# Decay factors of an mLSTM one step ahead, and an output projection that begins inside the last attention heads

## The reference, cut to what matters

```
# first block, mLSTM: 4 heads of 128 features, two directions (one direction shown)
qk  = einsum('bhcjd,bhcsd->bhcjs', q, k)
P   = exp(D - m_j[..., None]) * qk
num = einsum('bhcjs,bhcsd->bhcjd', P, v) + inter_w * einsum(C_prev, q)
h   = num / maximum(abs(den), exp(-m_j))
h   = h * rsqrt(mean(h * h) + EPS) * norm_g            # per head
# second block, forgetting attention: 16 heads of 64 features, causal
s = einsum('bhqd,bhkd->bhqk', q_i, k) * scale + c_i[..., None] - c
o = einsum('bhqk,bhkd->bhqd', softmax(where(kpos <= qpos, s, -inf)), v)
o = o * sigmoid(gate)
x = x + o @ b_w_out                                    # "bout" below
```

## Time and profile before

| | us |
|---|---|
| median of 3 runs (2162.28 to 2163.73) | 2163.47 |
| the profiled execution's own time | 2162.06 |
| its span, first to last instruction | 2160.3 |
| PE busy in the span | 2115.6 (98%) |
| POOL, DVE, ACT busy | 1208.9, 962.1, 881.5 |

### The profile page before, as it was taken

One profiled execution on the slowest core, in us unless ns is written; L12 is line 12 of the kernel. 1 busy time (PEld: TensorE's weight loads), 2 busy tenths in 40 slices (PEclk: granted clock), 3 DMA queues, 4 the chain that ended last, 5 costly groups with the idle time before them and its releaser, 6 DMA issues.

```text
span 2160.3 us, 29709 instructions
## 1 busy us (share of the span) xinstructions
PE 2115.6 (98%) x9884; PEld 1716.2 (79%) x9884; DVE 962.1 (45%) x1675; ACT 881.5 (41%) x1325; POOL 1208.9 (56%) x1601
## 2 busy tenths in 40 slices
PE   8999998999999999999999999999999989999999
PEld 6787877887888888888788888887777768888887
DVE  5557455335444442224445555115556554555400
ACT  5444456333443433332244343225545544444321
POOL 7454335778566565654556556566444436565653
PEclk9999999999999999999999999999999999999999
DMA  6233211333333323332333333333222213333332
GB/s 218 94 93 112 67 59 54 88 93 99 97 106 91 102 88 107 96 101 88 94 91 97 97 97 93 99 100 118 69 89 88 69 40 98 101 93 97 99 99 74
DMA packets 60827, 202.88 MB, mean 94 GB/s; under 512 B 6768, under 2 KB 6896, under 8 KB 60736
## 3 DMA queue, kind: packets, MB, share of 16 engines
q1 hardware_dynamic: 60624, 201.55, 30.8%
q10 hardware_dynamic: 112, 0.16, 0.0%
HBM read 199.42 MB, written 2.26 MB: 93 GB/s over the span
## 4 chain that ended last, share of the span: by engine, by line
PE 89%; DVE 4%; ACT 3%; DVEq 1%; issue 1%; ACTq 1%; POOL 1%; DMA 0%; SPq 0%; POOLq 0%
PE bank L1483 27%; PE bank L1485 27%; PE bank L1484 27%; PE bank L1734 1%; PE bank L1708 1%; PE bank L1720 1%; PE bank L1771 1%; ACTq L665 1%; PE bank L1772 1%; PE bank L1773 1%; PE bank L1527 1%; POOL WL L472 1%; PE bank L1752 1%; DMA X<-in_x 0%; ACT SX L664 0%
## 5 line engine op out<-in xcount | busy, mean ns | idle before, releaser
L472 POOL TENSOR_TENSOR WL<-RAW,WH 128x256 fp32r<-128x256 f32 x1496 | 1160.6, 809 | 893.9 <-ACT WH L579 893.3
L1483 PE MATMUL bank<-XH,WH 128*128 128x512 f32 x1816 | 715.5, 394 | 2.8 <-DVE VN L1196 2.5
L1485 PE MATMUL bank<-XH,WL 128*128 128x512 f32 x1816 | 707.9, 390 | 0.0
L1484 PE MATMUL bank<-XL,WH 128*128 128x512 f32 x1816 | 707.6, 390 | 0.0
L579 ACT ACTIVATE WH<-RAW 128x1024 fp32r<-128x1024 f32 x374 | 392.0, 1051 | 240.1 <-PE bank L1485 237.6
L1483 PEld LDWEIGHTS bank<-XH,WH 128*128 128x128 f32 x1816 | 341.3, 188 | 82.9 <-DVE FG L1402 4.5
L1485 PEld LDWEIGHTS bank<-XH,WL 128*128 128x128 f32 x1816 | 341.3, 188 | 71.6
L1484 PEld LDWEIGHTS bank<-XL,WH 128*128 128x128 f32 x1816 | 341.5, 188 | 71.1 <-issue 1.4
L1483 PE MATMUL bank<-FH,WH 128*128 128x512 f32 x528 | 205.4, 389 | 0.0
L1485 PE MATMUL bank<-FH,WL 128*128 128x512 f32 x528 | 205.4, 389 | 0.0
L1484 PE MATMUL bank<-FL,WH 128*128 128x512 f32 x528 | 205.4, 389 | 0.0
(11 more groups left out here) (274 smaller groups left out, 2373.6 us busy)
## 6 DMA issues: line engine op xcount, KB each, us to landing
RAW<-in_w_up SPq DMA_DIRECT2D x132, 512.0 KB, 3.6
RAW<-in_w_att SPq DMA_DIRECT2D x50, 512.0 KB, 3.6
RAW<-in_w_down SPq DMA_DIRECT2D x48, 448.0 KB, 3.3
RAW<-in_w_fa SPq DMA_DIRECT2D x32, 512.0 KB, 3.6
RAW<-in_w_down SPq DMA_DIRECT2D x24, 512.0 KB, 3.5
RAW<-in_w_ain SPq DMA_DIRECT2D x24, 512.0 KB, 3.6
RAW<-in_w_mrg SPq DMA_DIRECT2D x15, 512.0 KB, 3.6
RAW<-in_w_mrg SPq DMA_DIRECT2D x24, 256.0 KB, 2.6
```

Of the source, the lines that this page charges most:

```text
L472: last = nc.gpsimd.tensor_tensor(WL[:, s, w], RAW[:, s, w], WH[:, s, w].bitcast(F32), ALU.subtract)
L1483: mm(dst[:, 0:width], WH[:, s, w], a, start=start and k == 0, stop=False)
L1484: mm(dst[:, 0:width], WH[:, s, w], b, start=False, stop=False)
L1485: last = mm(dst[:, 0:width], WL[:, s, w], a, start=False, stop=stop and k == kc - 1)
```

## The change

1. `SXM` has its two tiles the other way round, and ACT makes the decay factors of step m+1 where it made those of step m. Those of step 0 are made in the slot of the last cross-attention step.
2. The last 128 columns of `bout` units 0 to 3 (their last part) go to tiles of their own, `WEH` (ACT) and `WEL` (POOL). ACT's `hi` for these units is two instructions, POOL's `lo` five. `bout_ends` reads the new tiles.
3. A new semaphore `bout_read` counts when part 6 of unit n has been read; ACT then copies units 4 to 7 (`hi_behind`) while the last pair is still in work. The residual no longer does it (`have = 5`).
4. PE's fillers are cut: unit 1 in parts 0-1 and 2-5, unit 2 in 0-2 and 3-6, unit 3 in 0-3 and 4-6, part 6 of units 0 and 1 earlier; the transposes of the last group stand ahead of unit 3, no longer behind it. Units 1 and 2 exchange their banks.
5. DVE: `o_gate` and `o_split` of pair 6 move behind the work of groups 0 and 1 of pair 7; ACT follows (`o_split`, and `out_gate` of pair 7 one group later). The first six `o_split` are dealt 4 and 2, no longer 3 and 3.

```
@@ -245,3 +245,3 @@
     EG = [at(f"EG{n}", k, [P, S]) for n, k in enumerate((74, 76, 78, 80, 82, 84, 54, 56, 58))]
-    SXM = [SX, at("SX1", 86, [P, 2, S])]
+    SXM = [at("SX1", 86, [P, 2, S]), SX]
@@ -267,2 +267,5 @@
     CD = at("CD", 86, [P, 2, 2, P])
+    WEH = at("WEH", 80, [P, 4, P], F32R)
+    WEL = at("WEL", 82, [P, 4, P], F32R)
+    KEND = (KB - 1) * P
@@ -312,3 +315,3 @@
     f_mask = sem("f_mask")
-    oh_ready, ol_ready = sem("oh_ready"), sem("ol_ready")
+    oh_ready, ol_ready, bout_read = sem("oh_ready"), sem("ol_ready"), sem("bout_read")
     out_done = sem("out_done")
@@ -359,3 +362,3 @@
-    BOUT = [bank[7], LB[(O["bout"] + 1) % 2], LB[O["bout"] % 2], bank[2], bank[3], bank[4], bank[5], bank[6]]
+    BOUT = [bank[7], LB[O["bout"] % 2], LB[(O["bout"] + 1) % 2], bank[2], bank[3], bank[4], bank[5], bank[6]]
@@ -553,8 +556,17 @@
                     f_masks((n - 6 - g) // 4, g)
-        lo(U["bout"], 0, 0, 0)
+        def lo_parted(n):
+
+            s = (U["bout"] + n) % NSLOT
+            pool.wait_ge(hi_ready, U["bout"] + n + 1)
+            for w in [slice(c * 2 * P, min((c + 1) * 2 * P, KEND)) for c in range(LO_PARTS)]:
+                nc.gpsimd.tensor_tensor(WL[:, s, w], RAW[:, s, w], WH[:, s, w].bitcast(F32), ALU.subtract)
+            nc.gpsimd.tensor_tensor(WEL[:, n, :], RAW[:, s, KEND:UW], WEH[:, n, :].bitcast(F32), ALU.subtract)\
+                .then_inc(lo_ready, 1)
+
+        lo_parted(0)
         f_masks(FA_LAST - 1, 2)
-        lo(U["bout"], 1, 0, 0)
-        lo(U["bout"], 2, 0, 0)
+        lo_parted(1)
+        lo_parted(2)
         f_masks(FA_LAST, 0)
-        lo(U["bout"], 3, 0, 0)
+        lo_parted(3)
         f_masks(FA_LAST, 1)
@@ -650,5 +662,6 @@
                        accum_out=RS[:, turn_of(g, j)]).then_inc(p_exp, 1)
-            if st and st[0] == "ml":
-                h, s = st[1], st[2]
-                m = 4 * h + s
+            m = 0 if st == LAST_STEP else 4 * st[1] + st[2] + 1 if st and st[0] == "ml" else 4 * ML_H
+            if m < 4 * ML_H:
+
+                h, s = m // 4, m % 4
                 if s == 0:
@@ -657,5 +670,5 @@
                     act.wait_ge(v_ready, VEV[("gate", 0)] + 1)
-                if m < 2:
+                if m == 1:
                     act.wait_ge(t_full, 2 * len(STEPS))
-                else:
+                elif m >= 2:
                     act.wait_ge(ms_read, m - 1)
@@ -750,3 +763,3 @@
                 for j in range(per):
-                    if not (at_end and j + AHEAD >= per) and not (have and i == 0 and j < have):
+                    if not (at_end and j + AHEAD >= per) and not (have and i * per + j < have):
                         hi(U[name], j + AHEAD, i, per)
@@ -834,2 +847,19 @@
+        def hi_parted(n):
+
+            s = (U["bout"] + n) % NSLOT
+            act.wait_ge(raw_full[s], 16 * ((U["bout"] + n) // NSLOT + 1))
+            act.wait_ge(unit_done, U["bout"] + n - NSLOT + 1)
+            if n == 0:
+                act.wait_ge(fc_out, 16)
+            A_(WH[:, s, 0:KEND], RAW[:, s, 0:KEND], ACT.Copy)
+            A_(WEH[:, n, :], RAW[:, s, KEND:UW], ACT.Copy).then_inc(hi_ready, 1)
+
+        def hi_behind(n):
+
+            s = (U["bout"] + n) % NSLOT
+            act.wait_ge(raw_full[s], 16 * ((U["bout"] + n) // NSLOT + 1))
+            act.wait_ge(bout_read, n - NSLOT + 1)
+            A_(WH[:, s, :], RAW[:, s, :], ACT.Copy).then_inc(hi_ready, 1)
+
         def squared(p, s):
@@ -881,6 +911,8 @@
             for s in range(4):
-                if p < FA_PAIRS:
+                if p < FA_PAIRS and 4 * p + s + AHEAD < 4 * FA_PAIRS:
                     hi(U["fa"], 4 * p + s + AHEAD, 0, 0)
+                elif p < FA_PAIRS:
+                    hi_parted(4 * p + s + AHEAD - 4 * FA_PAIRS)
                 elif s == 0:
-                    hi(U["bout"], AHEAD, 0, 0)
+                    hi_parted(AHEAD)
                 if p < FA_LAST and s >= 2:
@@ -891,7 +923,11 @@
                     head_rstd(FA_LAST, 1)
-                    o_split(FA_LAST - 1)
                 if p >= 1 and s < FA_G:
                     exps(p - 1, s)
-                if p >= 1 and s == 0:
+                if 1 <= p < FA_PAIRS and s == 0:
                     out_gate(p - 1)
+                if p == FA_PAIRS:
+                    if s == 0:
+                        o_split(FA_LAST - 1)
+                    for n in ((), (4, 5), (6,), (7,))[s]:
+                        hi_behind(n)
                 if p < FA_PAIRS and (s == 0 or s == (2 if p == FA_LAST else 1)):
@@ -903,4 +939,6 @@
                     turned(p - 1, s)
+                if p == FA_PAIRS and s == 1:
+                    out_gate(FA_LAST)
                 if p == FA_LAST and s >= 2:
-                    for n in range(3 * s - 6, 3 * s - 3):
+                    for n in range(4) if s == 2 else range(4, FA_LAST - 1):
                         o_split(n)
@@ -908,3 +946,3 @@
         fa_rounds(round_)
-        residual("bout", 2, 4, 4, "fg2", unrolled=lambda j: None, have=1)
+        residual("bout", 2, 4, 4, "fg2", unrolled=lambda j: None, have=KB - AHEAD)
         up("up2", 2, 11, ACT.Silu)
@@ -1417,4 +1455,2 @@
                 head_done(FA_LAST, 1)
-                o_gate(FA_LAST - 1)
-                o_split(FA_LAST - 1)
                 values_out(FA_LAST)
@@ -1422,3 +1458,7 @@
                     mins(FA_LAST, g)
+                    if g == 1:
+                        o_split(FA_LAST - 1)
                     shares(FA_LAST, g)
+                    if g == 0:
+                        o_gate(FA_LAST - 1)
                 o_gate(FA_LAST)
@@ -1767,3 +1807,3 @@
             for k in range(k0, k1):
-                if n == 0:
+                if n == 0 or k == FA_LAST - 1:
                     pe.wait_ge(ol_ready, k + 1)
@@ -1775,16 +1815,15 @@
                 last.then_inc(unit_done, 1)
+            elif k1 == KB - 1 and n < NSLOT:
+                last.then_inc(bout_read, 1)
-        def bout_ends(count):
+        def bout_ends():
             k = KB - 1
-            w = slice(k * P, (k + 1) * P)
             pe.wait_ge(oh_ready, KB)
-            for n in range(count):
-                slot = (U["bout"] + n) % NSLOT
-                mm(BOUT[n][:], WH[:, slot, w], AH[:, k, :], start=False, stop=False)
-                mm(BOUT[n][:], WL[:, slot, w], AH[:, k, :], start=False, stop=False)
+            for n in range(NSLOT):
+                mm(BOUT[n][:], WEH[:, n, :], AH[:, k, :], start=False, stop=False)
+                mm(BOUT[n][:], WEL[:, n, :], AH[:, k, :], start=False, stop=False)
             pe.wait_ge(ol_ready, KB)
-            for n in range(count):
-                slot = (U["bout"] + n) % NSLOT
-                mm(BOUT[n][:], WH[:, slot, w], AL[:, k, :], start=False, stop=True).then_inc(unit_done, 1)
+            for n in range(NSLOT):
+                mm(BOUT[n][:], WEH[:, n, :], AL[:, k, :], start=False, stop=True).then_inc(unit_done, 1)
@@ -1796,8 +1835,12 @@
                 f_turn(pp)
+                pe.wait_ge(lin_free, O["bout"] + 1)
+                bout(1, 0, 2)
                 f_scores(pp, 0)
-                pe.wait_ge(lin_free, O["bout"] + 2)
-                bout(1, 0, pp)
+                bout(1, 2, pp - 1)
                 f_transposes(pp, 0)
                 f_scores(pp, 1)
-                bout(2, 0, pp)
+                pe.wait_ge(lin_free, O["bout"] + 2)
+                bout(2, 0, 3)
+                bout(0, pp - 1, pp)
+                bout(1, pp - 1, pp)
                 f_products(pp, 0)
@@ -1805,9 +1848,10 @@
                 f_scores(pp, 2)
+                bout(2, 3, pp)
                 f_products(pp, 1)
-                pe.wait_ge(fs_read, 2 * FA_G * FA_PAIRS - 1)
-                bout(3, 0, pp)
                 f_transposes(pp, 2)
-                bout(0, pp - 1, pp)
+                pe.wait_ge(fs_read, 2 * FA_G * FA_PAIRS)
+                bout(3, 0, 4)
                 f_products(pp, 2)
-                bout_ends(4)
+                bout(3, 4, pp)
+                bout_ends()
                 pe.wait_ge(fo_free, FA_PAIRS)
```

## The result

| | before | after |
|---|---|---|
| median of 4 runs each, us | 2162.88 (2161.14 to 2163.73) | 2143.08 (2141.58 to 2143.14) |
| profiled execution, its span | 2162.06, 2160.3 | 2143.13, 2141.4 |

The ratio is 0.9906 (95% interval 0.9894 to 0.9918): 19.8 us or 0.94% faster. Predicted were 2143.9 us and a span of 2140.7.

The account below looks back on a forecast made before the run. PE bounds the kernel, busy 2115.6 of 2160.3 us, so only idle time can be won. 10.5 (mLSTM) and 9.1 (last pair) sum to 19.6 us: span 2140.7, median 2143.9, own range 2141.5 to 2148, with rivals 1 and 2 to 2151.5.

Parts of the forecast that it names:

- mLSTM: PE's waits before the mLSTM products: 10.2 us plus nine times 0.16 won, less 0.3, 0.6 and 0.2, gives 10.5.
- third steps: Third step of each mLSTM head: waits closed with 0.3 us to spare, called thin; 0.3 charged over the heads.
- rival 1: GpSimd collides with DVE's group 2, residuals and mLSTM third steps: 6.3 us less gain, 2150.2; chance 0.17.
- entry: Last cross-attention step: step 0's factors ahead of four copies make these 0.8 late; 0.6 us paid, bounds 0 and 1.9.
- end: After mLSTM step 15: the head's normalisation starts from DVE's row as before, 0.2 us lost.
- The clock: Output projection: the fall of the clock goes with the 5.5 us wait before unit 4, 1.7 us won.
- The last pair: Last pair of heads and output projection: gross 11.0 us won, less 0.9, 0.5 and 0.5, gives 9.1.
- (a): Transposes of the last pair's group 2: a new wait of about 1 us, charged 0.9, bounds 0 and 3.3.
- (b): Last pair: five more switches between kinds of matmul, each between 0 and 0.16 us, charged 0.5.
- (c): Eight residuals before `up2`: margin 1.1 us less 0.2, eaten by GpSimd collisions; charged 0.5, bounds 0 and 3.
- 2: Output projection: unit 4's preparation doesn't get through, the 5.5 us wait and slow clock stay, 7.4 slower, 2151.3; chance 0.06.
- 3: mLSTM: DVE's masks fall on GpSimd's `WL` at 15 steps, 25.5 us lost against 19.6 won, 2169.4; chance 0.03.

Follow-up runs that it names:

- e6: Kernel after, with the factors of mLSTM step 0 behind the four copies of the last cross-attention step instead of ahead; 2141.32 us.
- e7: Kernel after, with the next step's factors ahead of the unit's `hi` in every mLSTM slot instead of behind it; 2141.35 us.
- e3: Kernel after, with output projection units 4 to 7 prepared late, in the residual, as before (takes back point 3); 2149.38 us.
- e9: Kernel before, unchanged, run once more for a second trace; 2162.87 us.
- e1: Kernel before with point 1 of the change alone (factors one step ahead, `SXM` swapped); 2153.49 us.
- e2: Kernel after with point 1 undone, so the last pair's changes alone; 2152.61 us.
- e10: Kernel after with point 1 undone, run once more for a second trace; 2152.71 us.
- e5: Kernel after, unchanged, run once more for a second trace; 2143.72 us.
- e4: Kernel after, with DVE's three `y_lo` instructions of units 8 to 10 one slot later; 2140.20 us.
- e8: Kernel after with three edits: `y_lo` one slot later, step 0's factors behind the copies, factors ahead of `hi`; 2139.11 us.

## Why the prediction was right, step by step

**mLSTM, 10.5 predicted.** Section M won 1407.4 - 1398.0 = 9.4 with a half-clock stretch in it that before's trace lacked. e6, the same steps without that stretch, has 1396.5: 10.9. Less the 0.3 at the entry it is 10.6, against the 10.5 of the sum. This agreement has some luck in it, as its terms show. First and second steps closed, as worked out: `PT` started at 266.57 where some 266.7 was set, and of its idle time that ended on `SX` 0.2 us are left of 36.8. The *third steps* were called thin, with 0.3 charged. They kept 0.30 and 0.46, and e7 shows 1.2 in all, with the cause that rival 1 named: a mask beside GpSimd, though at 0.67 to 0.81 us and not 1.38. The criterion "no wait over 0.3" failed by that; "total under 1" held (0.8). The *entry* was over-sized: it cost 0.3 where 0.6 was set, though the row shows 0.60. The *end* was under-sized: 0.2 predicted, 1.81 against 1.36 measured, so 0.4 to 0.5. The closed waits, each with its 0.16, less what is left and the two costs give some 0.9 less than was measured. Short idle times, which the waits of PE don't list, may have gone as well; no run assigns them.

**The clock, 1.7 counted as won.** The 1.7 was my estimate from the earlier trace rows: half of the 3.4 us in which the clock was 0.55 and 9 matmuls stand where 17 stand later. No run shows that number: before gives 1.6, e3 2.0. At its place the term is right: with the wait the slow clock goes, and e3 brings both back. From the matmul behind the wait to the end of L before takes 23.4 us and after 21.8, so it was worth 1.6. As a term of the whole sum it is the step that failed. I took the one trace of before to have all its stretches and none to be added. After has one at 373 us that this trace of before lacks; it costs 1.5 (M of after and of e6), and it is more than the 0.7 by which the span missed 2140.7. The median doesn't show it: it fell by 19.8, the span by 18.9. Most executions of before are at a mean clock of 0.997, its first profile at 0.998. They probably pay for one more stretch, as e9 (0.997) does in the mLSTM section, but there are no traces of them.

**The last pair, 9.1 predicted, 9.4 measured** (L 10.2 shorter, U 0.85 longer).
(a) The transposes of group 2 were to wait 0.9. They wait 0.10 and 0.15, and e3, without the two `hi`, gives back 0.2. I had ACT's gate 1.3 us behind the point at which the exponentials could start. In after it is 0.3:

```profile
1738.69 2.00 ACT L863 ACTIVATE WH<-RAW 128x1024 fp32r<-128x1024 f32 x2 [1.00 <-PE bank L1813]
...
1742.99 0.28 DVE L1413 CUSTOM_DVE_ANT_0 FX<-bank,CD 128x128 f32<-128x128 f32 x1
...
1743.06 0.63 ACT L889 ACTIVATE FG<-FG 128x512 f32<-128x512 f32 x1
1743.60 0.49 ACT L898 ACTIVATE FX<-FX,NX 128x256 f32<-128x256 f32 x1
...
1746.52 0.55 PE L1760 MATMUL bank<-IDN,FX 128*128 128x128 f32 x3 [0.15 <-DVE FX L1428]
```

The minima end at 1743.28 and the exponentials start at 1743.60, 4.9 after the release at 1738.69, not 5.5; the minima themselves come at 4.6, not 4.2.
(b) The switches, 0.5: the three waits that the fillers closed were 3.3 us, 3.7 with 0.16 each. e3 against e9 shows 3.2 won, so some 0.5 went for switches and whatever else stands beside the fillers. L is 10.2 shorter where 11.0 - 0.9 - 0.5 = 9.6 was predicted: 0.7 more by (a), 0.1 less by the clock.
(c) The residuals, 0.5 predicted, 0.85 measured by section U (e3 takes it away). `up2` waits 0.56 for the eighth, on `XL`. That was named as a sign of being wrong, though the sum charged 0.5 for just this. The sixth of them shows the collision that had been left for the upper bound:

```profile
1770.65 0.75 DVE L1282 SCALAR_TENSOR_TENSOR XL<-X,PAR,XH 128x512 fp32r<-128x512 f32 x1
...
1773.31 0.69 DVE L1279 TENSOR_TENSOR SS<-SS,SQ 128x512 f32<-128x512 f32 x1 [1.31 <-ACT SQ L777]
1773.92 1.23 DVE L1282 SCALAR_TENSOR_TENSOR XL<-X,PAR,XH 128x512 fp32r<-128x512 f32 x1
...
1782.70 0.50 PE L1523 MATMUL bank<-XH,WH 128*128 128x512 f32 x1 [0.56 <-DVE XL L1282]
```

`XL` takes 1.23 beside GpSimd's `WL` and 0.75 one turn earlier, where `WL` starts only at 1771.04. The seventh and eighth take 1.23 as well. Three times 0.48 is 1.4, against a margin of 1.1 less 0.2: this leaves the 0.5 that `up2` waits.

**The rivals.** 1 (collisions of DVE and GpSimd, 2150.2): they are there at the third steps (1.2 us, by e7) and in (c) (0.85), 2 us in all; their size, 6.3 on top of what the forecast had charged, is not. A mask there takes 0.81 us beside GpSimd's `WL` in after and 0.28 with GpSimd idle in e7; what holds it up, no run shows. 2 (the preparation doesn't get through, 2151.3): no; its price, which e3 shows, is 6.6 in the trace where 7.4 was set, since (c) gives 0.85 back. 3 (slower, 2169.4): no; its condition came in part. `PB`'s mask takes 0.81 to 0.83 us in eleven of the 16 steps, where it did so in two before, but only two of these steps keep a wait.

## What to carry to other kernels

An idle engine that "waits for X" may wait for what stands ahead of X in X's queue: making ACT's factors a step earlier, `YL` a slot later and the factors ahead of `hi` took 10.6, 1.3 and 1.2 us off sections of equal clock without removing one instruction. When resources of a stage that is nearly finished (here a slot of `WH`) hold back the next, cut off the last small piece that holds them. 128 columns in tiles of their own, and with them an early start of the next units, gave 6.6 us. And take a profile's clock stretches as one draw: before a difference of 1 to 2 us is given to an edit, compare the same matmuls in two traces of each kernel. The start of the program alone varies by 3 us here.

## What was not expected of the hardware

A stretch of 3.4 us at half clock costs 1.2 to 1.6 us here: 1.6 at 73 us (matmuls 201 to 301 take 21.8 to 21.9 us in the nine traces with it, 20.3 in the three without), 1.2 at 361 (M of e9 and of before), 1.4 at 1732 (L of e1 and of e9), 1.5 at 373 (M of after and of e6). It belongs to no wait for certain. Of the traces in the table, the 2.55 us wait near 72 us had one behind it in nine of twelve (not in e2, e7 and e9). The 2.2 us wait at 360 us had one in two of four (e2 and e9, not before and e10), the 1.8 us wait behind the mLSTM steps in five of eight (after, e1, e3, e5, e7; not e2, e6, e9), waits of 0.9 and 1.5 close together in one of three (e1). The 5.5 us wait had one in all four. With the wait behind the mLSTM steps at 1.36 (before, e10) or cut to 0.35 (e4, e8) none came.

Other waits as long never had one: 2.2 us at the last head's first step (343 us) in none of four traces, 1.7 us between 1061 and 1075 us in none of twelve. So length alone does not decide. What else does is open: two executions of one program differ (behind the 2.2 us wait at 360 us the clock was 0.56 in e9 and 1.00 in before), and no run here shows why.

And closing a wait gives more than its listed length at some places (M, by 0.9) and less at others (the entry, 0.3 of 0.6).
